# A Hymba-style layer on one Trainium2 core: new in-order sequences for the Strassen units and plain downs, and fewer accumulating weight transfers

## What is computed

```python
def _half_ffn(x, norm_g, w_gate, w_up, w_down):
    h = _rmsnorm(x, norm_g)
    return x + 0.5 * ((jax.nn.silu(h @ w_gate) * (h @ w_up)) @ w_down)

xp = _half_ffn(xp, ffn1_norm[l], ffn1_w_gate[l], ffn1_w_up[l], ffn1_w_down[l])
...
xp = xp + mixed @ w_out[l]
xp = _half_ffn(xp, ffn2_norm[l], ffn2_w_gate[l], ffn2_w_up[l], ffn2_w_down[l])
```

## Time and profile before

| what | value |
|---|---|
| device time, median of 3 runs | 916.34 us (912.33 to 917.66) |
| the profiled execution's own time | 918.1 us |
| its span, first to last instruction | 916.3 us |
| mean granted TensorE clock | 0.992 |
| PE busy | 867.6 us (95%) |
| DVE busy | 689.3 us (75%) |
| ACT busy | 436.2 us (48%) |
| POOL busy | 89.1 us (10%) |

### The profile page before, as it was taken

The page is one execution under the profiler, slowest core; times in us unless marked ns, Lnnn a source line. Parts: engine busy times, 40 slices in busy tenths (PEclk is TensorE's granted clock), DMA queues, the critical chain, the costliest instruction groups (busy, mean ns, idle before and its releaser), DMA issues.

```text
span 916.3 us, 17091 instructions
## 1 busy us (share of the span) xinstructions
PE 867.6 (95%) x6943; PEld 848.0 (93%) x6943; DVE 689.3 (75%) x1046; ACT 436.2 (48%) x702; POOL 89.1 (10%) x84
## 2 busy tenths in 40 slices
PE   9999989998999997999999999998899979999888
PEld 8998989998999997999889999998899979999888
DVE  7976788887888864755885887857888778887744
ACT  8632355545545542434753575423554455554410
POOL 0000011111111100013332001000111111111000
PEclk9999999999999998999999999999999999999989
DMA  8122666686757731422301517227665867677221
GB/s 306 48 82 69 199 158 145 148 199 180 169 122 189 194 83 56 177 84 79 124 25 60 170 61 204 63 70 222 159 152 125 221 171 156 133 197 194 70 93 70
DMA packets 62799, 124.27 MB, mean 136 GB/s; under 512 B 5345, under 2 KB 20833, under 8 KB 62721
## 3 DMA queue, kind: packets, MB, share of 16 engines
q1 hardware_dynamic: 48208, 98.16, 33.6%
q0 software_dynamic: 12784, 22.55, 16.3%
q10 hardware_dynamic: 1728, 2.48, 0.7%
HBM read 119.22 MB, written 3.60 MB: 134 GB/s over the span
## 4 chain that ended last, share of the span: by engine, by line
PE 73%; DVE 14%; issue 5%; DMA 4%; ACT 3%; SPq 1%; DVEq 0%; ACTq 0%
PE ps L757 16%; PE ps L878 14%; PE ps L880 14%; PE ps L879 14%; PE ps L960 10%; DMA full<-gu 4%; DVE wlo L1806 4%; DVE hlo L1927 3%; PE ps L1129 1%; PE ps L1111 1%; ACT whi L1363 1%; DVE hfull L1913 1%; PE ps L1120 1%; DVE gate L1862 1%; ACT u2c L1379 1%
## 5 line engine op out<-in xcount | busy, mean ns | idle before, releaser
L878 PE MATMUL ps<-xhi,whi 128*128 128x260 f32 (+1 forms) x1092 | 313.9, 287 | 35.8 <-ACT u2c L1379 23.2
L879 PE MATMUL ps<-xlo,whi 128*128 128x260 f32 (+1 forms) x1092 | 310.9, 285 | 0.0
L880 PE MATMUL ps<-xhi,wlo 128*128 128x260 f32 (+1 forms) x1092 | 310.5, 284 | 0.0
L878 PEld LDWEIGHTS ps<-xhi,whi 128*128 128x128 f32 x1092 | 205.9, 189 | 41.9 <-issue 28.8
L1806 DVE TENSOR_TENSOR wlo<-full,whi 128x1024 fp32r<-128x1024 f32 (+1 forms) x165 | 210.8, 1305 | 0.0
L880 PEld LDWEIGHTS ps<-xhi,wlo 128*128 128x128 f32 x1092 | 206.5, 189 | 0.0
L879 PEld LDWEIGHTS ps<-xlo,whi 128*128 128x128 f32 x1092 | 206.3, 189 | 0.0
L879 PE MATMUL ps<-hlo,whi 128*128 128x268 f32 (+1 forms) x336 | 95.5, 284 | 0.0
L880 PE MATMUL ps<-hhi,wlo 128*128 128x268 f32 (+1 forms) x336 | 95.4, 284 | 0.0
L878 PE MATMUL ps<-hhi,whi 128*128 128x268 f32 (+1 forms) x336 | 95.4, 284 | 0.0
L2398 POOL DMA_DIRECT2D full<-gu x31 | 37.4, 1207 | 455.2 <-DMA full<-gu 455.2
(11 more groups left out here) (220 smaller groups left out, 1522.8 us busy)
## 6 DMA issues: line engine op xcount, KB each, us to landing
full<-gu SPq DMA_DIRECT2D x78, 512.0 KB, 4.7
full<-gu POOLq DMA_DIRECT2D x31, 512.0 KB, 6.1
full<-d SPq DMA_DIRECT2D x32, 384.0 KB, 3.7
full<-gu SPq DMA_DIRECT2D x39, 256.0 KB, 4.5
full<-d POOLq DMA_DIRECT2D x16, 384.0 KB, 5.3
full<-d SPq DMA_DIRECT2D x8, 768.0 KB, 4.2
raw<-w_in SPq DMA_DIRECT2D x10, 512.0 KB, 3.8
raw<-gu SPq DMA_DIRECT2D x8, 512.0 KB, 3.9
```

The lines of the kernel that those rows point to most:

```text
L878: nc.tensor.matmul(dst, whi_t, mhi_t, start=(first and pr == 0), stop=False, skip_group_check=True)
L879: nc.tensor.matmul(dst, whi_t, mlo_t, start=False, stop=False, skip_group_check=True)
L880: last = nc.tensor.matmul(dst, wlo_t, mhi_t, start=False, stop=(pr == pairs - 1), skip_group_check=True)
```

## The change

On TensorE P2 goes ahead of P5 in every unit, the first output of a plain down is cut differently around P3' and P4', and in part 3 the last weight tile of output 0 moves behind five of output 1. On ScalarE hi_b and (from the next unit) hi_c are made a unit ahead, hi_b ahead of silu_1 and u2c, and silu_0 goes last. On VectorE weight_lo 1 is made a unit ahead, weight_sums goes ahead of take_chain, pair_lo and pair_sums go behind make_hid and ahead of take_single, and make_std moves to the first unit. Whole weights are loaded and split once P6 of the slot's old unit is done (before: P4), and the first two loads of a Strassen unit are issued together. Accumulating transfers stay for spread units and tiles 7 to 17 where two Strassen units stand before; tiles 18 to 21 and, in stage 2, tiles 3 to 5 get VectorE's add. `whole_step` gathers VectorE's part of a whole unit. The diff, cut to its core:

```diff
             elif strassen(s, v - 1):
-                names = [("P1", v), ("P7", v), ("P3", v - 1), ("P6", v), ("P4", v - 1), ("P5", v), ("P2", v)]
+                names = [("P1", v), ("P7", v), ("P3", v - 1), ("P6", v), ("P4", v - 1), ("P2", v), ("P5", v)]
+PAIR_SPLIT = [FIRST[p] + i for p in (1, 2) for i in (3, 5, 7)]
 def sum_by_transfer(s, v):
-    return strassen(s, v) and v >= 2 and (strassen(s, v - 1) and strassen(s, v - 2))
+    return strassen(s, v) and strassen(s, v - 1) and strassen(s, v - 2) and not (PLAN[s][v][0] == "gate" and not FIRST[1] + AHEAD < PLAN[s][v][1] < FIRST[3] + AHEAD)
 def load_strassen(s, v):
             sp.dma_start(full[:, r, 1:5:3, 0:w], src[:, 2:3, :].to_broadcast([P, 2, w])).then_inc(c_loaded[r], 16)
-            if strassen(s, v - 3):
-                sp.wait_ge(products, product_no(s, v - 3, "P2"))
             sp.dma_start(full[:, r, 0:4:3, 0:w], src[:, 0:2, :]).then_inc(a_loaded[r], 16)
 def load_whole(s, v):
-                sp.wait_ge(products, product_no(s, v - 3, "P4"))
+                sp.wait_ge(products, product_no(s, v - 3, "P6"))
 # TensorE, units
                     if q == 0:
-                        down(s, v, 0, [0])
+                        down(s, v, 0, [0, 1])
                         p3(s, v - 1)
+                        down(s, v, 0, [2])
                         p4(s, v - 1)
-                        down(s, v, 0, list(range(1, t)))
+                        if unit[1] == 3:
+                            down(s, v, 0, list(range(3, t - 1)))
+                            down(s, v, 1, list(range(t - 1)))
+                            down(s, v, 0, [t - 1])
+                            down(s, v, 1, [t - 1])
+                            continue
+                        down(s, v, 0, list(range(3, t)))
+                p2(s, v)
                 p5(s, v)
-                p2(s, v)
 # ScalarE: d_split_hi waits for P6 in place of P4; units
                 if kind == "whole":
                     if q < 3:
                         d_split_hi(s, v + 1)
                     elif more:
                         hi_a(s, v + 1)
                         hi_b(s, v + 1)
+                        hi_c(s, v + 1)
+                    if q == 0:
+                        silu_1(s, v - 1)
+                        if unit[1] == 3:
+                            tile_hi(s, KF - 1)
-                if v:
-                    hi_c(s, v)
                 seed_p1(s, v)
                 if strassen(s, v + 1):
                     hi_a(s, v + 1)
+                    if pair_to_split(s, v) is not None:
+                        pair_hi(s, pair_to_split(s, v))
+                    hi_b(s, v + 1)
+                else:
+                    d_split_hi(s, v + 1)
                 if u_before and PLAN[s][v - 1][0] == "gate":
                     silu_1(s, v - 1)
                 keep_u2(s, v)
                 if v == 0:
                     t4_hi(s, STAGES[s]["n"])
+                if kind == "gate" and f in (FIRST[1] + 2, FIRST[2] + 2):
+                    move_tile(s, f - 2)
+                    move_tile(s, f - 1)
+                if strassen(s, v + 1):
+                    hi_c(s, v + 1)
+                tiles_hi(s, v)
+                if kind == "gate":
+                    silu_0(s, v)
 # VectorE
+        def whole_step(s, v):
+            _, p, q = PLAN[s][v]
+            if q < 3:
+                d_split_lo(s, v + 1)
+            elif v + 1 < len(PLAN[s]):
+                weight_sums(s, v + 1)
+                weight_lo(s, v + 1, 0)
+            if q == 0:
+                take_chain(s, v - 1)
+                ...
+                take_up0(s, v - 1)
+                make_hid(s, v - 1)
+                if p == 3:
+                    tile_lo(s, KF - 1)
+            ...
+            add_down(s, p, 2 * q)
+            if s == 0 and p == 3:
+                next_tile(2 * q)
+            if q == 3 and v + 1 < len(PLAN[s]):
+                weight_lo(s, v + 1, 1)
+            ...
+                add_down(s, p, 2 * q + 1)
 # VectorE, units
                 if v:
-                    weight_lo(s, v, 1)
                     weight_lo(s, v, 2)
-                if f in (FIRST[1] + 3, FIRST[1] + 5, FIRST[1] + 7, FIRST[2] + 3, FIRST[2] + 5, FIRST[2] + 7):
-                    pair_lo(s, f - 3)
+                if strassen(s, v + 1):
+                    weight_sums(s, v + 1)
+                else:
+                    d_split_lo(s, v + 1)
                 if u_before:
                     take_chain(s, v - 1)
                 if strassen(s, v + 1):
-                    weight_sums(s, v + 1)
                     weight_lo(s, v + 1, 0)
-                else:
-                    d_split_lo(s, v + 1)
+                    weight_lo(s, v + 1, 1)
                 if v == 0:
+                    make_std(s)
                     t4_lo(s, STAGES[s]["n"])
                 if u_before:
                     take_up0(s, v - 1)
                     ...
+                if kind == "gate" and f in PAIR_SPLIT:
+                    pair_lo(s, f - 3)
+                if kind == "gate" and f + 1 in PAIR_SPLIT:
+                    pair_sums(s, f - 1)
                 take_single(s, v)
-                if v == 1:
-                    make_std(s)
```

More of the change, by code:

```diff
@@ L1445, in pair_to_split @@
             kind, f = PLAN[s][v][0:2]
[L1446 to L1450, removed]
+            return f - 3 if kind == "gate" and f in PAIR_SPLIT else None
         def units(s):
             for v, unit in enumerate(PLAN[s]):
+                kind, f = unit[0:2]
                 u_before, more = strassen(s, v - 1), v + 1 < len(PLAN[s])
@@ L1457, in units @@
                     keep_u4(s, v - 1)
-                if unit[0] == "whole":
+                if kind == "whole":
                     q = unit[2]
[L1460 to L1463, removed]
                     if q < 3:
@@ L1472, in units @@
                     continue
-                if v:
-                    hi_c(s, v)
                 seed_p1(s, v)
-                if pair_to_split(s, v) is not None:
-                    pair_hi(s, pair_to_split(s, v))
                 if strassen(s, v + 1):
                     hi_a(s, v + 1)
+                    if pair_to_split(s, v) is not None:
[3 more added lines that the diff above has]
+                    d_split_hi(s, v + 1)
                 if u_before and PLAN[s][v - 1][0] == "gate":
@@ L1484, in units @@
                     t4_hi(s, STAGES[s]["n"])
+                if kind == "gate" and f in (FIRST[1] + 2, FIRST[2] + 2):
+                    move_tile(s, f - 2)
+                    move_tile(s, f - 1)
                 if strassen(s, v + 1):
-                    hi_b(s, v + 1)
-                else:
-                    d_split_hi(s, v + 1)
-                if unit[0] == "gate":
+                    hi_c(s, v + 1)
+                tiles_hi(s, v)
+                if kind == "gate":
                     silu_0(s, v)
-                if unit[0] == "gate" and unit[1] in (FIRST[1] + 2, FIRST[2] + 2):
-                    move_tile(s, unit[1] - 2)
-                    move_tile(s, unit[1] - 1)
-                tiles_hi(s, v)
         def end_down(s, d):
@@ L1999, in last_down, with next_tile @@
                                         ).then_inc(x_added, 1)
+        def next_tile(d):
+            if d >= 6:
+                split_lo(U_IN + d - 6)
+            dve.wait_ge(x_added, x_updates(0, 3) + d + 1)
+            x_lo(xlo[:, d, :], xhi[:, d, :], d, d, 1, 0, NH_ALL)
+            if d:
+                add_square(1, d, 0, NH_ALL)
+        def whole_step(s, v):
[7 more added lines that the diff above has]
+                take_chain(s, v - 1)
+                if p == 0:
+                    x_to_std(s, 0)
+                    x_to_std(s, 1)
+                take_up0(s, v - 1)
+                make_hid(s, v - 1)
+                if p == 3:
+                    tile_lo(s, KF - 1)
+            elif p == 0:
+                x_to_std(s, 2 * q)
+                x_to_std(s, 2 * q + 1)
+            add_down(s, p, 2 * q)
[3 more added lines that the diff above has]
+                weight_lo(s, v + 1, 1)
+            if s and p == 3 and q == 3:
+                last_down()
+            else:
+                add_down(s, p, 2 * q + 1)
+            if s == 0 and p == 3:
+                next_tile(2 * q + 1)
@@ L2001, in units @@
         def units(s):
[L2003 to L2004 removed]
+            for v, (kind, f, *_) in enumerate(PLAN[s]):
+                u_before = strassen(s, v - 1)
                 if u_before:
                     take_up1(s, v - 1)
[L2007 to L2037 removed]
@@ L2038, in units @@
+                if kind == "whole":
+                    whole_step(s, v)
                     continue
-                f = unit[1] if unit[0] == "gate" else None
                 if v:
-                    weight_lo(s, v, 1)
                     weight_lo(s, v, 2)
-                if f in (FIRST[1] + 3, FIRST[1] + 5, FIRST[1] + 7, FIRST[2] + 3, FIRST[2] + 5, FIRST[2] + 7):
```

(10 more changed lines are left out.)

47 lines of the change are left out of this document (5 added, 42 removed).

## The result

The changed kernel takes 878.2 us (median of 4 runs, 875.3 to 880.0), the kernel before in the same session 917.0 (912.3 to 918.4): a ratio of 0.958, 95% interval 0.954 to 0.963. The forecast was 882. The profiled execution of after took 875.3 us (span 873.6) and is the fastest of its four; against the profiled execution of before, 918.1, it has 42.8 us less, on the medians it is 38.8.

The account below looks back on a forecast made before the run. TensorE's stalls and clock bound the kernel: 49.2 us lost in stalls less 19.9 left is 29.3, plus 5.3 of clock, 34.6 won. Profiled 918.1 becomes 883.5, median 882; range 871 to 897, with 0.72 on 874 to 889.

Parts of the forecast that it names:

- u2c at tile 6: Tile 6 of both stages: P5 still waits for ScalarE's copy u2c, as sums come late; 1.25 and 1.4 us.
- first units: The first units of the stages keep u2c stalls of 0.15, 0.15 and 0.45 us.
- xT at tile 6: xT stalls at tile 6 stay, since add_down 6 stands behind sums and weight_lo: 0.8 and 1.5 us.
- reciprocal: make_std's 3.49 us pass in each stage's first unit makes the first P3' wait: 2.5 and 2.6 us.
- output 2: Last plain downs: output 2 waits for VectorE's two passes on output 0; about 0.95 us lost per stage.
- tile 18: Last spread unit ahead of tile 18: VectorE's added work makes the next P1 wait; 0.4 and 0.6 us.
- tile 12, stage 2: Tile 12's unit in stage 2: late accumulating transfer costs 2.9 us, and 1.8 more in the units after it.
- VectorE's round: VectorE's work in two successive units just fits: 20.2 against TensorE's 20.8, stage 2 19.9 against 20.2; 1.5 us charged.
- the rival's condition: VectorE's round binds if each of 12 passes costs 0.08 more or each handover 0.5 more; 890 us; chance 0.14.
- The rival that transfers are late everywhere: Gate units: landings after 5.9 us stall P5, up0 and the next P1; slower, up to 971 us; chance 0.04.
- The half clock behind the reciprocal: Sign of being wrong: half clock returns behind the 2.6 us stalls that make_std's pass causes in the first units.
- my 5.3: TensorE time lost to half clock behind stalls at each stage's end, 2.7 and twice 1.3 us, expected won back.

Follow-up runs that it names:

- e_both_back: Changed kernel with P5 ahead of P2 again and pair_lo ahead of the chain again: 895.4 us, ratio 0.975.
- b_pair_lo_late: Kernel before with one edit, VectorE does pair_lo behind make_hid instead of ahead of the chain: 897.2 us, ratio 0.977.
- e_round_longer: Changed kernel with one unused VectorE pass added ahead of take_single in the 22 gate units of tiles 7 to 17: 888.9 us, ratio 0.970.
- e_transfers_back: Changed kernel with accumulating transfers back in the eleven gate units that had got VectorE's add: 877.8 us, ratio 0.958.
- b_downs: Kernel before with only the change's TensorE order in the plain downs: 908.8 us, ratio 0.992.
- e_all: Changed kernel with make_std behind tile 5's chain, x_to_std 6 and 7 earlier, output 0's late tile behind three of output 1: 866.4 us, ratio 0.943.
- e_pair_lo_first: Changed kernel with pair_lo directly ahead of the chain again: 880.2 us, ratio 0.958.
- e_x67_early: Changed kernel with VectorE's passes x_to_std 6 and 7 moved ahead of add_down 5: 875.0 us, ratio 0.953.
- e_p5_first: Changed kernel with TensorE doing P5 ahead of P2 again, the a load waiting for P2 as before: 884.4 us, ratio 0.962.

## Why the prediction was right, and where it was off

Each term of the sum for what is left, and what the trace of after shows (start-to-start loss, us):

| term | forecast | after |
|---|---|---|
| u2c at tile 6 | 2.65 | 0.91 + 1.04 |
| first units | 0.75 | under 0.4 |
| xT at tile 6 | 2.3 | 0.81 + 0.91 |
| reciprocal | 5.1 | 2.34 + 2.32 |
| output 2 | 1.9 | 1.15 + 1.13, and 0.54 at a later output of stage 1 |
| tile 18 | 1.0 | 0.22 + 0.43 |
| tile 12, stage 2 | 4.7 | 0.35 |
| VectorE's round | 1.5 | 0.31 + 0.30 |
| sum | 19.9 | 13.2 |

**The main steps held.** Odd tiles: all u2c stalls gone for the reason given (e_both_back, b_pair_lo_late), though I did not see that either of the two orders would do it alone. The reciprocal's price was right to 0.3 us a stage, and so was output 2's to 0.2. The downs' stalls went with their half clock. "It just fits" was right for VectorE's round, and e_round_longer shows how closely; the rival's condition, 0.08 more on each pass, is not met there (0.61 from start to start for a pass of 0.69). The rival that transfers are late everywhere fell: eleven more of them change nothing on the whole (e_transfers_back). The five wlo stalls (5.5 us lost in the trace of before) are gone too, as forecast. That weight_lo 1 a unit earlier is what removed them is argued, not shown alone: they stand unchanged at 4.7 us of idle in b_pair_lo_late and b_downs, and no run undoes that move.

**The mis-sized term** is tile 12 in stage 2, 4.7. It was built from one late landing, to which I added a delay as if that landing were fixed. It is not: in the table it costs 0.3 to 2.5, 1.55 on the mean of seven traces, it comes at tile 12 rather than at tile 13 as before, and its follow-on cost stays nearly all in the one P5 and the next P1. The right term was 1.5 with bounds 0.3 and 2.5. Why it lands on time in some executions is open. The order of products and loads seems to bear on which transfer is late: with the old order tile 13's took 8.6, 8.7 and 7.9 us to land in three traces of five (before, b_pair_lo_late, e_both_back; in b_downs it is tile 12's with 7.8), with the new order 5.6 to 6.3 in the seven of the table, and tile 12's is late in five of them. Whether the time of the broadcast load does this, and which way, no run shows.

**Smaller misses.** The wait of 0.54 at a later output of stage 1's part 3 was not forecast; it goes with e_all's order (0.27 there). The half clock behind the reciprocal was named as a sign of being wrong and is in no sum; it came in stage 1 and not in stage 2 of this execution, and cost 1.4 there (16 matmuls in 3.41 us where 28 fit). The old half clock may have been worth more than my 5.3: the spans of the two traces differ by 42.7, the losses in the stalls that the profile lists by 37.3 (49.2 less 11.9), so 5.4 are left for clock and small gaps, and 6.8 with the new stretch; the two are not told apart. Two of my figures are off by arithmetic alone: 10 x 0.12 is 1.2 and not 1.3, and 18.7 scaled by 7.52/7.69 is 18.3 and not 18.4; neither moves the forecast by more than 0.2. Forecast 34.6 gained; 38.8 on the medians and 42.8 between the two profiled executions, of which the second happened to have the transfer on time. The misses lie mostly on one side, too much charged, so little of the agreement comes from errors that cancel; with 1.5 for the transfer the same sum would have given 878.8.

## What to carry over

An operation that only a later unit needs (pair_lo) does not belong ahead of one that the next product waits for; look for it in the engine that the named waiter itself waits for, since u2c was ScalarE's but the cause was VectorE's. Two remedies for one stall often don't add, so undo them one by one and together before ranking them. And a single late transfer in one trace is a draw from a spread: give such a term its bounds from several traces, or take the transfer out where the loads are densest.

## What the hardware showed that I had not expected

- The granted clock does not follow from the idle time alone. Five traces have the reciprocal's stalls of 2.16 to 2.18 us in both stages (after, e_pair_lo_first, e_transfers_back, e_round_longer, e_x67_early): 3.41 us at 0.50 (1.2 of 2.4 GHz) follow soon in three of them in stage 1 and in two in stage 2, and in e_round_longer in neither. Stalls of 2.23 and 2.33 left the profiled execution of e_p5_first at 1.000; 2.21 and 2.31 at the same places of e_both_back were each followed by such a stretch. So was one of 1.81 in b_downs, while 2.59 at the end of b_pair_lo_late was not. Executions of one kernel differ as well: the other three of e_p5_first show 0.994 to 0.998 and took about 4 us longer. What tells them apart is not shown.
- Of the 302 accumulating transfers of 512 KB in the FFN stages of all thirteen traces, about four in five land 5.5 to 6.4 us after their issue. The seven over 8 us (up to 8.7) all belong to tiles 12, 13 and 19 in stage 2, among the first two behind four short spread units. The loads beside such a one can be slow as well (a broadcast load of 6.5 us in e_pair_lo_first, against a median of 4.5 for loads of that size in after). Which of these places has the late one, and whether any has, changes from trace to trace.
